# The first head's first eight picks from an 8x8 grid, gathered ahead of its other eight

## What is computed

```python
def peer_ffn(h, w_q, sub_keys, u, v):
    q = (ht @ w_q).reshape(T, PEER_HEADS, 2, PEER_QDIM // 2)
    s = jnp.einsum('thpd,pnd->thpn', q, sub_keys).astype(jnp.float32)
    top_s, top_i = lax.top_k(s, PEER_TOPK)
    cand_s = top_s[:, :, 0, :, None] + top_s[:, :, 1, None, :]
    cand_i = top_i[:, :, 0, :, None] * PEER_NKEYS + top_i[:, :, 1, None, :]
    best_s, best_j = lax.top_k(cand_s.reshape(T, PEER_HEADS, -1), PEER_TOPK)
    experts = jnp.take_along_axis(cand_i.reshape(T, PEER_HEADS, -1), best_j, axis=-1)
    gates = jax.nn.softmax(best_s, axis=-1)
...
        act = jax.nn.gelu(jnp.einsum('cd,ced->ce', xc, u[ec]))
        return jnp.einsum('ce,ced->cd', gc.astype(xc.dtype) * act, v[ec])
```

## Time and profile before

| | us |
|---|---|
| median of 3 runs | 2345.89 |
| lowest, highest | 2345.32, 2346.78 |
| profiled execution, its own time | 2341.84 |
| span of that execution | 2340.1 |
| busy in the span: PE | 1889.3 (81%) |
| DVE | 1337.5 (57%) |
| POOL | 555.0 (24%) |
| ACT | 326.8 (14%) |
| moved by the gathers | 536.90 MB |
| moved by the plain loads | 356.25 MB |

### The profile page before, as it was taken

How to read it: one execution, slowest core, us unless ns; L and a number is a source line. 1 busy time by engine, 2 the same in 40 slices (tenths; PEclk the granted TensorE clock), 3 DMA queues, 4 the chain that set the end, 5 groups by cost and what they waited for, 6 DMA issues and landing times. The chain is left out here.

```text
span 2340.1 us, 24801 instructions
## 1 busy us (share of the span) xinstructions
PE 1889.3 (81%) x9231; PEld 1012.9 (43%) x9231; DVE 1337.5 (57%) x3278; ACT 326.8 (14%) x822; POOL 555.0 (24%) x568
## 2 busy tenths in 40 slices
PE   6998766666679799988877777799989888777776
PEld 4665433333367464444322222285645443233322
DVE  3633000000065658767877886656677678778866
ACT  1052000000021430010000000113310100000001
POOL 1000000000000114434444343200234344344332
PEclk9999888888889899999999999999999999999999
DMA  9987999999997459999999999896599999999997
GB/s 397 424 265 281 430 428 429 428 430 428 427 338 309 183 229 409 421 421 421 417 421 418 416 413 422 355 364 243 228 422 421 421 419 421 412 416 413 410 422 325
DMA packets 119160, 894.80 MB, mean 382 GB/s; under 512 B 18460, under 2 KB 30588, under 8 KB 31868
## 3 DMA queue, kind: packets, MB, share of 16 engines
q0 software_dynamic: 73728, 536.90, 55.5%
q1 hardware_dynamic: 45308, 356.25, 37.5%
HBM read 889.68 MB, written 3.42 MB: 382 GB/s over the span
## 5 line engine op out<-in xcount | busy, mean ns | idle before, releaser
L2010 PE MATMUL psum<-sb_area 128*128 128x512 f32 x2048 | 978.3, 615 | 238.6 <-DVE sb_area L2765 234.3
L2791 DVE CUSTOM_DVE_ANT_0 sb_area<-sb_area 128x1024 f32<-128x1024 f32 x512 | 626.1, 1224 | 275.5 <-DMA sb_area<-in_peer_uv,sb_peer_e 273.2
L824 POOL DMA_INDIRECT sb_area<-in_peer_uv,sb_peer_e x512 | 537.3, 1049 | 1002.9 <-PE psum L2010 734.1
L2010 PEld LDWEIGHTS psum<-sb_area 128*128 128x128 f32 x2048 | 375.1, 193 | 721.3 <-DVE sb_area L2765 375.3
L1660 PE MATMUL psum<-sb_area 128*32 128x256 f32 x2048 | 171.5, 508 | 130.8 <-DMA sb_area<-in_moe_w_gu 128.8
L2293 DVE COPY sb_area<-psum 128x128 f32<-128x128 f32 x32 | 9.3, 292 | 391.3 <-PE psum L1672 391.3
L1242 ACT ACTIVATE sb_small<-sb_small 128x2 f32<-128x2 f32 x258 | 52.5, 203 | 1144.6 <-DVE sb_small L2791 1144.6
L2765 DVE SCALAR_TENSOR_TENSOR sb_area<-sb_ident,sb_small,sb_area 128x128 f32<-128x128 f32 x512 | 156.8, 347 | 52.9 <-ACT sb_small L1242 48.2
L1359 PE MATMUL psum<-sb_area 128*128 128x256 f32 x784 | 176.2, 387 | 3.2 <-DVE sb_area L2127 3.2
L1660 PEld LDWEIGHTS psum<-sb_area 128*32 128x32 f32 x2048 | 82.2, 144 | 219.8 <-DMA sb_area<-in_moe_w_gu 142.8
L804 POOL TENSOR_SCALAR_AFFINE_SELECT sb_area<-sb_area 128x256 f32<-128x256 f32 x1 | 0.4, 406 | 726.2 <-DVE sb_area L2597 726.2
(11 more groups left out here) (376 smaller groups left out, 1364.0 us busy)
## 6 DMA issues: line engine op xcount, KB each, us to landing
sb_area<-in_moe_w_gu SPq DMA_DIRECT2D x30, 4096.0 KB, 33.4
sb_area<-in_ada_w SPq DMA_DIRECT2D x72, 1024.0 KB, 12.3
sb_area<-in_moe_w_dn SPq DMA_DIRECT2D x32, 2048.0 KB, 23.9
sb_area<-in_peer_w_q_runs SPq DMA_DIRECT2D x8, 2048.0 KB, 12.4
sb_area<-in_sb_w_in_runs SPq DMA_DIRECT2D x6, 2048.0 KB, 21.6
sb_area<-in_odd_w_in_runs SPq DMA_DIRECT2D x6, 2048.0 KB, 10.9
sb_area<-in_even_w_in_runs SPq DMA_DIRECT2D x5, 2048.0 KB, 12.3
sb_area<-in_moe_w_gu SPq DMA_DIRECT2D x4, 2048.0 KB, 21.4
```

Source lines behind the costliest of these rows:

```text
L824: pool.indirect_dma_start(uv_rows[s], None, rows, bass.IndirectOffsetOnAxis(ap=peer_e[:, m:m + 1], axis=0)).then_inc(named(f"uv_loaded{s}" ...
L2010: last = pe.matmul(ps[:, 4 + 2 * t + half, :], diag[:, s, :], uv_rows[s][:, D + half * HALF:D + (half + 1) * HALF], start=(k == 0), stop=( ...
L2791: dve.tensor_tensor_reduce(uv_rows[s][:, 0:D], uv_rows[s][:, 0:D], h_tok[:, m // P, :], 1.0, 0.0, ALU.mult, ALU.add, dots[:, m % BODY:m % ...
```

## The change

`FEW = 8` is added. In both layers the first call of `find_picks` (head 0 of tile 0) becomes two functions. `first_picks` takes the 8 best keys of each side, adds an 8 x 8 grid (into the unused second head's part of `cand`), takes the best 8 of its 64 sums and looks them up with 64 comparisons a side in place of 256; it adds one to `experts_made`. `further_picks` strikes out the keys found, takes the next 8, adds the whole 16 x 16 grid, strikes the 8 sums found out of its 8 x 8 corner, takes the best 8 of the 256, and looks these up with 128 comparisons a side; it adds one more to `experts_made`. POOL waits for the first count ahead of m = 0 and for the second ahead of m = 8. What follows on DVE is as before.

```diff
--- before.py
+++ after.py
@@ -49,6 +49,7 @@
 
 PEER_HEADS = 8
 PEER_K = 16
+FEW = 8
 NKEYS = 128
 PEER_EXPERTS = NKEYS * NKEYS
 RING = 8
@@ -522,7 +523,7 @@
 
         def experts_at(L, m):
 
-            return (UNITS + 1) * L + (m // UNIT + 2 if m >= UNIT else m // PEER_K + 1)
+            return (UNITS + 2) * L + (m // UNIT + 3 if m >= UNIT else m // PEER_K + 2 if m >= FEW else 1)
         block = ctx.enter_context(nc.Block())
         ADA = [(I["ada_w"][0], 0), (I["ada_w_2"][0], KC), (I["ada_w_2"][1], KC)]
         BIAS_AT = [(0, 64), (1, 0), (1, 48)]
@@ -817,7 +818,7 @@
                     pool.wait_ge(named("pair_turned"), SECOND_AT + PAIRS_OF)
                 for m in range(T):
                     s = m % RING
-                    if m % UNIT == 0 or m == PEER_K:
+                    if m % UNIT == 0 or m in (FEW, PEER_K):
                         pool.wait_ge(named("experts_made"), experts_at(L, m))
                     if L * T + m >= RING:
                         pool.wait_ge(named("v_used"), L * T + m - RING + 1)
@@ -2634,8 +2635,7 @@
 
 
                     t, i = u // 4, u % 4
-                    half = count < GH
-                    dve.wait_ge(named("keys_copied"), keys_at(L, i, t) - (1 if half and first_head == 0 else 0))
+                    dve.wait_ge(named("keys_copied"), keys_at(L, i, t))
                     at = t * HP + GQ * i + 2 * first_head
                     nq, nk = 2 * count, count * PEER_K
                     rows = [(at + j, key_score[:, at + j, :], key_left[:, j, :]) for j in range(nq)]
@@ -2672,8 +2672,6 @@
                     yield
                     marked()
                     top = t * PEER_HEADS + GH * i + first_head
-                    if split and u == 0 and first_head == 0:
-                        dve.wait_ge(named("pair_weighed"), SECOND_AT + PAIRS_OF)
                     heads = [(top + h, first_head + h, cand[:, h, :], cand_left[:, h, :]) for h in range(count)]
                     for r, _, s, _ in heads:
                         last = dve.max(best[:, r, 0:8], s)
@@ -2766,8 +2764,86 @@
                                                         g.broadcast_to([P, P]), ALU.mult, ALU.mult)
                     last.then_inc(named("diag_made"), 1)
 
-                for _ in find_picks(0, 0, 1):
-                    pass
+                few_cand = cand[:, 1, 0:FEW * FEW]
+                few_grid = [P, FEW, FEW]
+                all_grid = cand[:, 0, :].rearrange("p (a b) -> p a b", b=PEER_K)
+
+                def pick_few(ranks, shift, mask, size):
+
+                    dve.tensor_scalar(best_hi[:, 0:FEW], best_at[:, 0, ranks], shift, None, ALU.logical_shift_right)
+                    mark(dve.tensor_scalar(best_lo[:, 0:FEW], best_at[:, 0, ranks], mask, None, ALU.bitwise_and))
+                    marked()
+                    dve.tensor_copy(best_row[:, 0:FEW], best_hi[:, 0:FEW])
+                    mark(dve.tensor_copy(best_col[:, 0:FEW], best_lo[:, 0:FEW]))
+                    marked()
+                    for side, place in ((0, best_row), (1, best_col)):
+                        last = dve.tensor_tensor(match[side][:, 0:FEW, 0:size], iota_16[:, 0:size].unsqueeze(1).broadcast_to([P, FEW, size]),
+                                                 place[:, 0:FEW].unsqueeze(2).broadcast_to([P, FEW, size]), ALU.is_equal)
+                    mark(last)
+                    marked()
+                    for side in range(2):
+                        hits = match[side][:, 0:FEW, 0:size]
+                        last = dve.tensor_tensor(hits, hits, key_num[:, side, 0:size].unsqueeze(1).broadcast_to([P, FEW, size]), ALU.mult)
+                    mark(last)
+                    marked()
+                    for side, pick in ((0, pick_i), (1, pick_j)):
+                        last = dve.tensor_reduce(pick[:, ranks], match[side][:, 0:FEW, 0:size], AX_X, ALU.add)
+                    mark(last)
+                    marked()
+                    mark(dve.scalar_tensor_tensor(pick_e[:, ranks], pick_i[:, ranks], float(NKEYS), pick_j[:, ranks], ALU.mult, ALU.add))
+                    marked()
+                    dve.tensor_scalar(peer_e[:, ranks], pick_e[:, ranks], float(L * PEER_EXPERTS), None, ALU.add
+                                      ).then_inc(named("experts_made"), 1)
+
+                def first_picks():
+
+                    dve.wait_ge(named("keys_copied"), keys_at(L, 0, 0) - 1)
+                    for side in range(2):
+                        last = dve.max(key_top[:, side, 0:FEW], key_score[:, side, :])
+                    mark(last)
+                    marked()
+                    dve.tensor_tensor(few_cand.rearrange("p (a b) -> p a b", b=FEW), key_top[:, 0, 0:FEW].unsqueeze(2).broadcast_to(few_grid),
+                                      key_top[:, 1, 0:FEW].unsqueeze(1).broadcast_to(few_grid), ALU.add)
+                    for side in range(2):
+                        last = dve.max_index(key_at[:, side, 0:FEW], key_top[:, side, 0:FEW], key_score[:, side, :])
+                    mark(last)
+                    marked()
+                    dve.tensor_copy(key_num[:, 0:2, 0:FEW], key_at[:, 0:2, 0:FEW])
+                    if split:
+                        dve.wait_ge(named("pair_weighed"), SECOND_AT + PAIRS_OF)
+                    mark(dve.max(best[:, 0, 0:FEW], few_cand))
+                    marked()
+                    mark(dve.max_index(best_at[:, 0, 0:FEW], best[:, 0, 0:FEW], few_cand))
+                    marked()
+                    pick_few(slice(0, FEW), 3, FEW - 1, FEW)
+
+                def further_picks():
+
+                    for side in range(2):
+                        last = dve.match_replace(key_left[:, side, :], key_top[:, side, 0:FEW], key_score[:, side, :], LOWEST)
+                    mark(last)
+                    marked()
+                    for side in range(2):
+                        last = dve.max(key_top[:, side, FEW:PEER_K], key_left[:, side, :])
+                    mark(last)
+                    marked()
+                    dve.tensor_tensor(all_grid, key_top[:, 0, :].unsqueeze(2).broadcast_to([P, PEER_K, PEER_K]),
+                                      key_top[:, 1, :].unsqueeze(1).broadcast_to([P, PEER_K, PEER_K]), ALU.add)
+                    for side in range(2):
+                        last = dve.max_index(key_at[:, side, FEW:PEER_K], key_top[:, side, FEW:PEER_K], key_left[:, side, :])
+                    mark(last)
+                    marked()
+                    dve.tensor_copy(key_num[:, 0:2, FEW:PEER_K], key_at[:, 0:2, FEW:PEER_K])
+                    mark(dve.match_replace(all_grid[:, 0:FEW, 0:FEW], best[:, 0, 0:FEW], all_grid[:, 0:FEW, 0:FEW], LOWEST))
+                    marked()
+                    mark(dve.max(best[:, 0, FEW:PEER_K], cand[:, 0, :]))
+                    marked()
+                    mark(dve.max_index(best_at[:, 0, FEW:PEER_K], best[:, 0, FEW:PEER_K], cand[:, 0, :]))
+                    marked()
+                    pick_few(slice(FEW, PEER_K), 4, PEER_K - 1, PEER_K)
+
+                first_picks()
+                further_picks()
                 if split:
                     residual_part(stage, 0, 1)
                 else:
```

## The result

The change made the kernel slower by about 0.2%: median 2349.41 us (2345.10 to 2355.11, 22 runs) against 2345.23 us for the kernel before in the same comparison (2341.62 to 2352.22, 22 runs), a ratio of 1.0019 with the 95% interval 1.0013 to 1.0025. That is +4.2 us where -1.2 was forecast. The profiled execution of the change took 2349.85 us (span 2348.0; before 2341.84 and 2340.1).

The account below looks back on a forecast made before the run. The peer loops wait for gathers, bounded by when each layer's gather stream starts running without a hole. Layer 0's +1.0 and layer 1's -2.2 sum to -1.2 us, from 2345.89 to 2344.7 us, range 2341.4 to 2347.8.

Parts of the forecast that it names:

- DVE's two pieces: Search on DVE: first piece 3.86 us, second 5.85, together 9.80 against 8.77, so later DVE work comes 1.0 us later.
- Layer 0, +1.0: Layer 0: DVE's delay passes down the chain to the ninth gather and the stream; +1.0 us, bounds 0 and +1.5.
- Layer 1, -2.2: Layer 1: earlier gathers fill idle DMA time, 1.1 us before 1664 and 1.1 to 1667; -2.2 us, bounds 0 and -4.8.
- DVE's delay: Layer 1: the 1.0 us goes into the second search's 2.77 us wait for key scores.
- The gathers' lead of 4.8 us pays nothing: Layer 0: gathers issued 4.8 us earlier gain nothing, since nothing waits for the first eight.
- the slower one: Layer 1: query weights wait behind eight gathers and PE waits for them; +10.7 us, 2357.6 with layer 0; chance 6%.
- The lost lead: Layer 1: PE's picks 2 to 5 free their slots no sooner; +1.0 us alone, 2346.9; chance 20%.
- the whole lead: Layer 1's stream starts the full 4.8 us sooner, 2342.1, chance 10%; in both layers 2336.3, chance 4%.
- the vanished wait at pick 4: Layer 1: sign that the first dot's 1.57 us wait for its gather at pick 4 would be gone.
- layer 0's ninth gather: Layer 0: it follows DVE's delay of 1.0 us; the forecast is wrong if it comes no later.
- PE's idle time before layer 1's pick 8: Layer 1: pick 8 had waited 2.11 us and can follow the lead; forecast wrong if it waits as long as before.
- The diagonals at 33.5: Layer 0: sign that the first diagonals come 33.5 us after the search's first MAX8, before 32.5.

Follow-up runs that it names:

- e1_dve_alone: The change with its whole VectorE search, but GpSimd starts no gather before the second count; ratio 1.0010 (1.0000 to 1.0020) to the kernel before.
- f3_layer0_only: The change in layer 0 alone, all eight gathers early, layer 1 as before; ratio 1.0008 (0.9998 to 1.0019) to the kernel before.
- f2_four_copy_four: The change, but between the first four gathers and the next four GpSimd waits for ScalarE's copy of the scores' second half; ratio 1.0004 to the kernel before.
- h1_four_copy_again: Four gathers, a wait for ScalarE's copy, then four, against the change, profiled again on a fifth chip; no ratio, stretches 653.0 / 655.9 us.
- e0_again: The changed kernel once more, unaltered, both layers with eight early gathers; ratio 1.0013 (1.0002 to 1.0023) to the kernel before.
- h2_change_beside: The whole change, unaltered, as control on the fifth chip; no ratio, stretches from first MAX8 to last issue 656.2 / 655.7 us.
- f1_layer1_two: Layer 0 as before; layer 1 has the changed search with two gathers ahead of the second count; ratio 0.9996 (0.9985 to 1.0007) to the kernel before.

## Why the prediction was wrong

- **DVE's two pieces**: right. 3.85 and 10.00 us against 3.86 and 9.80, and POOL's first gather 4.31 and 4.78 us after the first MAX8 (forecast 4.3 and 4.8).
- **Layer 0, +1.0**: right as a mechanism and short of most of the cost. Where the posts are prompt (`e1_dve_alone`, `f3_layer0_only`, `f2_four_copy_four`, `h1_four_copy_again`), the stretch is 653.3 us in the mean against 652.0 in five profiles of the old layer 0: +1.3, within the bounds given. Where they are late (seven profiles with eight early gathers) it is 656.1: +4.1. The two groups don't overlap (653.0 to 653.9 and 654.7 to 657.2), but they are not from the same chips. On one chip each, late less prompt is 1.4 us (`e0_again`, `e1_dve_alone`) and 3.2 us (`h2_change_beside`, `h1_four_copy_again`).
- **Layer 1, -2.2**: the size is right, its working only in part. Five profiles with an early lead and prompt posts have 656.0 us in the mean against 658.3 in four of the old layer 1: -2.2 before rounding, the forecast's size. The six with eight early gathers, late posts and the weight load in its place have 656.7: -1.5. DVE's delay was covered, as `e1_dve_alone` shows with 658.5. But on idle DMA engines the gathers' data came 1.6 us after the issue (1669.33 to 1670.96), and not 2.3, and the weights' first data did not come in its old place beside them but 11.0 us after the first MAX8, before 8.6. That these left -2.2 standing is in part luck.
- **The step that failed** is "The gathers' lead of 4.8 us pays nothing" in layer 0, with nothing set against it: an earlier row of gathers was priced at no cost for the other engines, and only its DMA time was followed. By the means above it costs 2.8 us in layer 0, by late posts of PE to ACT that the move put in front of a critical copy, and 0.7 of the gain in layer 1. Before, the row began at 852.50, when that copy was 0.5 us away, and the late posts fell behind it. Sum of the terms as measured: +4.1 - 1.5 = +2.6, where the three ratios of the whole change are +4.5, +3.0 and +0.7 us. What makes them differ stays open; in the first, the stretches of its own profile add up to +4.4. With prompt posts it would be +1.3 - 2.2 = -0.9, beside the -1.2 of the forecast. `f2_four_copy_four` is the nearest run to that, at +0.9 us with an interval from -1.4 to +3.0.
- **The rivals**: the slower one named a wait of PE for the weights. In the change it didn't happen: PE went on with them at 1690.00 straight behind its other work. But late posts had put PE back: it began 25.5 us after the first MAX8, before 19.2. Of the five profiles with an early lead and prompt posts, three have PE waiting for the weights, 0.25 us (`f1_layer1_two`), 0.29 (`f2_four_copy_four`) and 0.41 (`h1_four_copy_again`). So this rival was right in kind, and its 10.7 us far too large. The Trainium skill's "DMA: Bandwidth & Descriptors" (SWDGE vs HWDGE vs iDMA) has the two kinds of queue take turns. The trace of the change agrees once both move: from 855 to 858 us 0.42 MB of gathers went beside 0.82 MB of weights. It doesn't agree at the start: from 851 to 855 only weights moved (1.28 MB), though the first gather had been issued at 849.90. The lost lead and the whole lead are both refuted by layer 1's -2.2. No rival had the hand-off from PE to ACT in it, and the range ended 1.6 us below the measured median.
- **Signs given ahead**: POOL's start, DVE's pieces and the vanished wait at pick 4 came true. So did the two that would have shown the forecast wrong if absent: layer 0's ninth gather came later, by 5.2 us, and PE's idle time before layer 1's pick 8 was gone. The diagonals at 33.5 were seen only where the posts were prompt.

## What to carry to other kernels

When a row of transfers is moved earlier, lay its whole length beside the hand-offs of the other engines, not only beside the DMA engines' idle time: ask what each engine posts in the ten microseconds after the new start, and who waits for it. A wait that ends "remote" in the old profile, hidden or not, can be a price that moves onto the critical chain. If a lead is wanted only to fill a hole in the DMA engines, a few transfers are enough: two early gathers in layer 1 gave 2.2 us (656.1 and 656.0 against 658.3), and eight with late posts 1.5. The version that does so in layer 1 alone had the lowest ratio of these kernels in one of its two runs (0.9996 and 0.9989, about -1 and -2.6 us), though neither interval is clear of 1. There is little room for more: in one of the two its PE already waited 0.25 us for weights that came later than before.

## What the runs showed of the hardware

With eight indirect gathers that GpSimd issued early, one about every 1.25 us, posts of TensorE's matmuls whose recorded ends fell from 5.3 to 7.3 us after the first of them arrived 1.8 to 5.0 us late. It was so in 14 of 14 such starts of a layer outside one chip, in both layers, with and without a plain load beside the gathers. In the first profile of the change five posts of VectorE in the same 4.57 us came 0.01 us after the end of their instruction. The kernel before has such posts 5.0 and 5.4 us after its first gather in layer 0, 2.2 to 6.0 us late. There is one exception: in layer 0 of `e1_dve_alone` a post 5.0 us after the first of eight was prompt, on a chip on which the change's were late. With two early gathers the scores' posts were prompt, and in layer 1 also with four followed by a wait. One chip of the five on which experiments ran showed no late post. The mechanism stays open: the trace has no row for what holds the post back. It does show that held posts come out one behind the other, 0.05 and 0.06 us apart in layer 1 of the change.

In the change TensorE had 4.6 us without work, and its granted clock was 0.50 in the four microseconds after 862; in `e1_dve_alone`, after 1.36 us of waiting, it was 1.00.
